# Hybrid linear-attention and sliding-window block on one core: the value product of each attention job placed one product sooner, its second bank of scores exponentiated first, and the jobs' transfers moved in the queue

## The reference

```python
h = rmsnorm(x, g_pre)
q_a, k_a, v_a, lr_a, z_a, q_b, k_b, v_b, z_b, m_a, m_b = split(h @ w_in)
# branch A, gated linear attention: 4 heads, keys of 128, values of 256, chunks of 64 tokens
log_a = log_sigmoid(lr_a @ w_decay_up + b_decay_up) / 16
for each chunk:  S = S * exp(b_last) + (k * exp(b_last - b)).T @ v;   o = q @ S      # b = cumsum(log_a)
y_a = (rmsnorm(o_a, g_gla) * silu(z_a)) @ w_branch_gla
# branch B, attention: 16 heads of 64, 2 shared key heads, window of two chunks, rope, a learned sink
p = softmax(concat(q_b @ k_b.T / 8, sink))[..., :-1];   o_b = p @ v_b
y_b = (o_b * silu(z_b)) @ w_branch_swa
y = sigmoid(m_a + b) * y_a + sigmoid(m_b + b) * y_b
x = x + rmsnorm(y @ w_out, g_post)
```

## Time and profile before

| | |
|---|---|
| median of 3 runs | 1947.06 us (1942.76 to 1947.96) |
| the profiled execution, its own time | 1943.41 us |
| its span | 1941.5 us |
| TensorE matmul busy | 1859.3 us, 96% |
| VectorE busy | 1361.9 us, 70% |
| GpSimd busy | 1022.8 us, 53% |
| ScalarE busy | 814.8 us, 42% |

### The profile page before, as it was taken

One profiled execution on the slowest core, in us unless ns is written; L12 is line 12 of the kernel. 1 busy time (PEld: TensorE's weight loads), 2 busy tenths in 40 slices (PEclk: granted clock), 3 DMA queues, 4 the chain that ended last, 5 costly groups with the idle time before them and its releaser, 6 DMA issues. The chain is left out here.

```text
span 1941.5 us, 31399 instructions
## 1 busy us (share of the span) xinstructions
PE 1859.3 (96%) x11024; PEld 1478.0 (76%) x11024; DVE 1361.9 (70%) x2140; ACT 814.8 (42%) x1808; POOL 1022.8 (53%) x673
## 2 busy tenths in 40 slices
PE   8999989989999999999999999999999999999996
PEld 7877767777777767887877777777777777887885
DVE  6768866866788876647568877755888856446265
ACT  5456455433333444313246454543443444225431
POOL 5534445554444556734534555555454467538955
PEclk9999989999999999999999999999999999999998
DMA  7534375677888777877843365666887786775873
GB/s 277 136 96 138 122 219 162 178 213 207 218 213 257 226 207 233 276 261 264 230 141 127 106 185 165 157 168 156 211 245 234 219 257 232 250 229 193 279 253 118
DMA packets 474463, 391.20 MB, mean 201 GB/s; under 512 B 292836, under 2 KB 365092, under 8 KB 460996
## 3 DMA queue, kind: packets, MB, share of 16 engines
q1 hardware_dynamic: 474307, 389.20, 67.3%
HBM read 256.45 MB, written 132.64 MB: 200 GB/s over the span
## 5 line engine op out<-in xcount | busy, mean ns | idle before, releaser
L1008 PE MATMUL pu<-a_hi,w_hi 128*128 128x512 f32 x1824 | 729.1, 402 | 30.1 <-DVE ct L1842 12.2
L1008 PE MATMUL pu<-a_lo,w_hi 128*128 128x512 f32 x1824 | 713.1, 393 | 0.0
L1008 PE MATMUL pu<-a_hi,w_lo 128*128 128x512 f32 x1824 | 712.3, 393 | 0.4 <-POOL w_lo L1991 0.4
L1991 POOL TENSOR_TENSOR w_lo<-t,w_hi 128x512 fp32r<-128x512 f32 x256 | 357.3, 1405 | 418.7 <-ACT w_hi L1327 418.7
L1991 POOL TENSOR_TENSOR w_lo<-w_raw,w_hi 128x512 fp32r<-128x512 f32 x264 | 399.8, 1524 | 268.1 <-ACT w_hi L1327 268.0
L1008 PEld LDWEIGHTS pu<-a_hi,w_hi 128*128 128x128 f32 x1824 | 345.7, 190 | 138.0 <-issue 60.2
L1008 PEld LDWEIGHTS pu<-a_hi,w_lo 128*128 128x128 f32 x1824 | 346.1, 190 | 75.5 <-POOL w_lo L1991 0.8
L1008 PEld LDWEIGHTS pu<-a_lo,w_hi 128*128 128x128 f32 x1824 | 346.4, 190 | 68.0
L1327 ACT ACTIVATE w_hi<-t 128x512 fp32r<-128x512 f32 x256 | 158.5, 628 | 356.5 <-DVE t L534 284.6
L1009 PE MATMUL pu<-a_hi,w_hi 128*128 128x512 f32 x544 | 212.2, 390 | 0.0
L1009 PE MATMUL pu<-a_hi,w_lo 128*128 128x512 f32 x544 | 211.7, 389 | 0.0
(11 more groups left out here) (177 smaller groups left out, 2336.9 us busy)
## 6 DMA issues: line engine op xcount, KB each, us to landing
w_raw<-in_w SPq DMA_DIRECT2D x81, 1024.0 KB, 6.2
va_d<-ct SPq DMA_DIRECT2D x128, 64.0 KB
qb_d<-ct SPq DMA_DIRECT2D x32, 256.0 KB
zb_d<-ct SPq DMA_DIRECT2D x32, 256.0 KB
q_s<-qb_d SPq DMA_DIRECT2D x32, 256.0 KB, 3.3
z_s<-zb_d SPq DMA_DIRECT2D x32, 256.0 KB, 3.1
gb_d<-gb SPq DMA_DIRECT2D x32, 256.0 KB, 2.9
za_d<-ct SPq DMA_DIRECT2D x128, 64.0 KB
```

Source lines behind the costliest of these rows:

```text
L1008: return nc.tensor.matmul(dst, weights, moving, start=start, stop=stop, skip_group_check=True)
L1991: TT(flat(w_lo[o.n % NWB][:, :, :]), src, as_f32(flat(w_hi[o.n % NWB][:, :, :])), ALU.subtract) \
```

## The change

In words:

1. `SWA_PV` goes from f+7 to f+6, and with it `prob_values` on TensorE and `gb` on VectorE. `SWA_Z` goes from f+5 to f+4, but `load_swa_z` now stands behind the slot's stores.
2. The exponentials of `pm[1]` are done first, and `exp_ok` counts twice a job: after `pm[1]` and after the sink. The value product waits for the first count of the next job.
3. `RB` goes from slots 92 and 96 to 90 and 94, and ScalarE's copy of it stands ahead of the exponentials.
4. In SP's loop the store of `gb` and the loads of linear attention stand at the slot's start. The store of `ga` is one slot later. Stores of `qk`, `v`, `mA`, `mB` and `out` tiles are one slot later.
5. GpSimd's multiply of `z_g` stands first in its slot, and VectorE's `ga` last in its slot.
6. The first loads of `gate_b` come up to four slots sooner, each with the waits that its buffer needs.

```diff
-SWA_Z = {first + 5: n for first, n in SWA.items()}
-SWA_PV = {first + 7: n for first, n in SWA.items()}
+SWA_Z = {first + 4: n for first, n in SWA.items()}
+SWA_PV = {first + 6: n for first, n in SWA.items()}
-RB = {92: 0, 96: 1}
+RB = {90: 0, 94: 1}
...
                 if j == 0:
-                    sp.wait_ge(rd_ok, 16 * (sb + 1))
-                    stored(group_no(sb, "mB", 3))
+                    if n == 0:
+                        stored(group_no(sb, "mB", 3))
+                        sp.wait_ge(rd_ok, 16 * sb + 15)
+                        sp.wait_ge(up_ok, 16 * sb + 16)
+                    elif n == 2:
+                        sp.wait_ge(rd_ok, 16 * (sb + 1))
...
-                if r - 10 in GLA:
-                    job = GLA[r - 10]
+                if r - 11 in GLA:
+                    job = GLA[r - 11]
...
+                if r - 2 in SWA_PV:
+                    job = SWA_PV[r - 2]
...
+                    sp.wait_ge(gb_ok, n + 1)
+                    go(gb_d[g * 512:(g + 1) * 512, t0:t0 + P].rearrange("(e p) t -> p e t", p=P), gb[:, :, :], gb_out)
+                if r + 3 in GLA:
+                    load_gla(sb, GLA[r + 3])
+                if r + 1 in GLA:
+                    load_gla_q(sb, GLA[r + 1])
+                if r - 6 in GLA:
+                    load_gla_z(sb, GLA[r - 6])
                 if r + 5 == min(SWA):
                     load_swa(sb, 0)
                 elif r + 3 in SWA and SWA[r + 3]:
                     load_swa(sb, SWA[r + 3])
                 if r - 1 in SWA:
                     load_swa_v(sb, SWA[r - 1])
-                if r in SWA_Z:
-                    load_swa_z(sb, SWA_Z[r])
-                for g, n in ((step(s, lag), n) for n, lag in ((3, 4), (0, 5), (2, 6), (1, 7))):
+                for g, n in ((step(s, lag), n) for n, lag in ((3, 5), (0, 6), (2, 7), (1, 8))):
                     if g and g.fast and g.kind in ("qk", "v", "mA", "mB", "out"):
                         store_tile(g, n)
...
+                if r in SWA_Z:
+                    load_swa_z(sb, SWA_Z[r])
...
-                if r - 1 in SWA_PV:
-                    job = SWA_PV[r - 1]
...
-                if r + 3 in GLA:
-                    load_gla(sb, GLA[r + 3])
-                if r + 1 in GLA:
-                    load_gla_q(sb, GLA[r + 1])
-                if r - 6 in GLA:
-                    load_gla_z(sb, GLA[r - 6])
...
                 for n in range(4):
-                    if e == n - 2:
+                    if e == (-6, -5, -2, -4)[n]:
                         load_gate_b(sb, 0, n)
...
             def scores(n):
-                pe.wait_ge(exp_ok, n)
+                pe.wait_ge(exp_ok, 2 * n)
...
             def prob_values(n):
-                pe.wait_ge(exp_ok, min(n + 2, 16 * (n // 16 + 1)))
+                pe.wait_ge(exp_ok, 2 * n + 3 if n % 16 < 15 else 2 * n + 2)
...
+                if sb == 0 and r in RB:
+                    act.wait_ge(rb_ok, 3 + RB[r])
+                    A(rb[:, RB[r], :], pm[4][:, :], ACT.Copy).then_inc(rb_sb_ok, 1)
                 if r in SWA:
...
-                    for hh in range(8):
-                        A(prob[b][:, :, hh, :], pm[hh // 4][:, (hh % 4) * P:(hh % 4 + 1) * P]
-                          .rearrange("p (j k) -> p j k", k=TB), ACT.Exp, bias=ntop[b][:, hh:hh + 1], scale=HD ** -0.5, accum_out=den[b][:, hh:hh + 1])
+                    for hh in (4, 5, 6, 7, 0, 1, 2, 3):
+                        ins = A(prob[b][:, :, hh, :], pm[hh // 4][:, (hh % 4) * P:(hh % 4 + 1) * P]
+                                .rearrange("p (j k) -> p j k", k=TB), ACT.Exp, bias=ntop[b][:, hh:hh + 1],
+                                scale=HD ** -0.5, accum_out=den[b][:, hh:hh + 1])
+                        if hh == 7:
+                            ins.then_inc(exp_ok, 1)
...
-                if sb == 0 and r in RB:
-                    act.wait_ge(rb_ok, 3 + RB[r])
-                    A(rb[:, RB[r], :], pm[4][:, :], ACT.Copy).then_inc(rb_sb_ok, 1)
```

More of the change, by code:

```diff
@@ L829, in _ @@
                            ga[j * TB:(j + 1) * TB, :, :], ga_out)
+                if r - 2 in SWA_PV:
+                    job = SWA_PV[r - 2]
+                    n = 16 * sb + job
+                    g, t = divmod(job, NT)
+                    t0 = sb * SB + t * P
+                    sp.wait_ge(gb_ok, n + 1)
[6 more added lines that the diff above has]
+                    load_gla_z(sb, GLA[r - 6])
                 if r + 5 == min(SWA):
@@ L1759, in _ @@
                     dve.wait_ge(ntop_ok, 2 * n + 1)
-                    dve.wait_ge(exp_ok, n)
+                    dve.wait_ge(exp_ok, 2 * n)
                     TT(sd[:, :], cs["sinks"][:, 8 * g8:8 * g8 + 8], ntop[n % 2][:, :], ALU.add).then_inc(ntop_ok, 1)
@@ L1764, in _ @@
                     d = den[n % 2]
-                    dve.wait_ge(exp_ok, n + 1)
+                    dve.wait_ge(exp_ok, 2 * n + 2)
                     link(TT(d[:, :], d[:, :], se[:, :], ALU.add))
@@ L1814, in _ @@
                     dve.wait_ge(st_ok, n + 1)
[L1815 to L1821, removed]
                 g, i = at(s)
@@ L1952, in _ @@
                     split_fill(SPLIT_AT[s])
+                if r - 9 in GLA:
+                    n = 16 * sb + GLA[r - 9]
+                    dve.wait_ge(o_t_ok, n + 1)
+                    dve.wait_ge(zg_ok, n + 1)
+                    dve.wait_ge(ga_out, 16 * NB * n)
+                    TT(ga[:, :, :].rearrange("p g t -> p (g t)"), o_n[:, :],
+                       z_g[:, :, :].rearrange("p g t -> p (g t)"), ALU.mult).then_inc(ga_ok, 1)
                 if s == NS - 2 or s == NS:
@@ L2017, in _ @@
                 sb, r = rel(s)
+                if r - 8 in GLA:
+                    n = 16 * sb + GLA[r - 8]
+                    pr = n % 16 // NT
+                    pool.wait_ge(gla_z_in, 16 * (n + 1))
+                    TT(z_g[:, :, :], z_g[:, :, :], gate_g[:, 16 * pr:16 * pr + 16].unsqueeze(2)
+                       .broadcast_to([P, 16, TB]), ALU.mult).then_inc(zg_ok, 1)
                 if s in LO_AT:
@@ L2047, in _ @@
                     p = prob[n % 2]
-                    pool.wait_ge(exp_ok, n + 1)
+                    pool.wait_ge(exp_ok, 2 * n + 2)
                     pool.wait_ge(den_ok, n + 1)
@@ L2051, in _ @@
                        .broadcast_to([P, NB, 8, TB]), ALU.mult).then_inc(p_ok, 1)
[L2052 to L2057, removed]
                 if s == NS - 1 or s == NS:
```

5 lines of the change are left out of this document (removed).

## The result

The changed kernel takes 1932.83 us (median of 6 runs, 1925.52 to 1935.68) against 1943.31 us for the kernel before (6 runs, 1939.47 to 1947.96). The ratio is 0.9942, 95% interval 0.9926 to 0.9959: 11 us faster. 29 to 33 us were forecast (1914 us against 1943 or 1947). The number lies inside the range of the prediction, beside what it called rival (a). The profiled execution took 1935.43 us, its span is 1933.6 us: 8.0 us less than before by profile.

A forecast was written before the change was run, and what follows sets the result against it. TensorE, with matmuls busy 96% of the span, and its waits were taken as the bound. Savings 14 + 0 - 3 + 14 + 6 = 31 us took 1943.41 to 1912.4; half of 3.65 added gave 1914 us, range 1896 to 1936.

The forecast's parts named there:

- rival (a): Whole kernel: VectorE and SP give back more of the gain, 7 us saved, 1938 us; chance 0.20.
- What bounds the kernel: Whole kernel: TensorE's own work, busy 96% of the span, and what keeps it waiting set the end.
- half a stretch: TensorE after longer waits: a removed wait also gives back half its half-speed work; 20.5 us lost in all.
- Linear attention: Edits 4 and 5, both blocks: `z_g` first and `ga` last put L1842 ahead; 14 us saved, bounds 5 and 19.
- The waits before slots 204 and 468: Linear attention: TensorE's waits for L1842, 3.8 and 2.9 us, would be gone.
- Attention after the first job: Edits 1 and 2, later jobs of each block: `gb` waits removed; 14 us saved, bounds 5 and 22.
- the one half-speed stretch that was allowed: Attention, 345 to 485 us: no granted clock of 0.50 there, or one stretch.
- The first job: First attention job of a block: keys late instead of `gb`; no change, bounds 5 saved in both blocks, 4 lost.
- the norm: Second block, edit 3: TensorE's spread waits 3.1 us, half-speed stretch behind; 3 us lost, bounds 0 and 5.
- yB: Gates and fills, edit 6: fill 3 to 6 us sooner, L1831 waits shrink; 6 us saved, bounds 0 and 9.
- the sign that I named for it: Later tile stores, costed at nothing: lost cover would show as VectorE waiting for `ct` stores.
- (c): Attention: the value product waits for the second bank in each of 30 jobs; slower, 1959 us; chance 0.05.

The follow-up runs named there:

- z_two: The changed kernel with two `z_g` buffers and the load of `z_g` one slot sooner, `z_g` still first in GpSimd's slot: ratio 0.9901 to the kernel before.
- zg_last: The changed kernel with GpSimd's `z_g` put back last in its slot, VectorE's `ga` left last: ratio 0.9894 to the kernel before.
- only_ga_last: The kernel before with one edit, VectorE's `ga` last in its slot: ratio 0.9940 to the kernel before.
- hx_99: The changed kernel with two `z_g` buffers and VectorE's instructions of the second block's norm one slot sooner: 1912.69 us, ratio 0.9841 to the kernel before.
- m_early: The changed kernel with the stores of `mA` and `mB` tiles put back one slot sooner: ratio 0.9951 to the kernel before.

## Why the prediction was wrong, by its steps

**What bounds the kernel.** Right: all the gains come out of TensorE's waits and its half-speed work. How a gain splits between the two differs from one execution to the next. In the profiled pair it is all clock, over all the executions mostly waits, so that the sum's habit of adding half a stretch to each removed wait can't be tested on one pair.

**Linear attention, -14 forecast, -2 measured (3.4 and -1.5 us gained): the step that failed.** The prediction put it: "`z_g` takes 1.04 us of GpSimd ahead of `w_lo`, which is needed four slots later, so it is hidden." I priced the instruction and not the wait in front of it. I had also noted that `z_g`'s load waits for `ga` of the job before "at the end of a slot now", and followed that to SP's stores but not to GpSimd. The runs showed 84.7 us of GpSimd standing in 30 waits (58.9 in 18 before), now ahead of the slot's `w_lo`; VectorE's work 5.4 and 4.2 us longer than in `z_two`, where the standing is 16.5; and ten waits for `k_g`, 12.4 us, which the prediction does not mention. The mechanism that was forecast for `ga` last is right: without `z_g` first the two stages gain 10.1 and 6.2 us in `zg_last` and 8.1 and 6.0 in `only_ga_last`, 16 and 14 together, and 14 was said. The waits before slots 204 and 468 went as said.

**Attention after the first job, -14 forecast.** By the trace 9.9 + 0.9 = 10.8; `gb` no longer waits anywhere, as said, and the one half-speed stretch that was allowed is there. It is mis-sized by the wait of 4.8 us before slot 104. That VectorE becomes the limit between 345 and 400 us was said, and priced at 5; that its instructions are 2.5 times as long beside GpSimd's was not seen, although `ga` took 1.68 us in the earlier trace rows. Timed by themselves, the edits 1 to 3 gave 5.4 us where -14 + 3 = -11 was forecast. The traces do not settle why this is less than the 8.4 that they show in the changed kernel; both carry an uncertainty of 3 us or so.

**The first job, 0; the norm, +3.** Right in size: up to slot 94 the span is 2.4 us longer. The wait of 3.3 us at slot 90 was forecast as 3.1, and the keys took `gb`'s place at slot 78. The half-speed stretch that was to follow the norm's wait is not in this profile; other profiles with the same wait have it (`zg_last` at 314.6 us, `hx_99` at 314.1). SP stood longer than I thought, until 265.52, not 260 to 263, since the `zB` store took longer to land.

**yB, -6 forecast, nothing measured.** The fill's two waits there (L1831, 2.7 and 2.6 us) fell to one of 1.2, and L1859 rose by 5.4. The later stores, costed at nothing, are the reason for the second, and the sign that I named for it (VectorE waiting for `ct` stores) is the row above. But they are not what took the 6 us: with `mA` and `mB` stored early again `m_early` was no faster.

**The rivals.** The result lies nearest to (a), 1938, whose words were that VectorE and SP give it back; VectorE did, but `z_g` first with GpSimd's wait was the trigger, and no rival named GpSimd. (c) did not come: of 30 value products three wait for the exponentials.

## What to carry to other kernels

When an instruction is moved to the front of an engine's slot, price the wait that it brings, not its own length: ask when its operand's buffer is freed, and by whom, after the other moves of the same change. A good move (`ga` last, worth some 11 us by itself) can be undone by one that looks free (`z_g` first) through one single-buffered tile; run the square of four. And when a removed wait comes back under another name three times over, the bound is a chain; look for what stretches its links. And before a gain is put down to the clock or to waits, look at the clock of more than one execution.

## What the runs showed of the hardware

- In one pair of profiles TensorE's waits stayed at 84.1 us against 82.2 and the kernel still became 8 us faster, because fewer stretches ran at 0.50 of the clock (27.2 us instead of 43.7). Executions of one and the same kernel have mean granted clocks from 0.982 to 0.989, so that a single pair can show several us of this that are not the change's.
- The same VectorE instruction with two inputs in SBUF takes 0.68 us alone and 1.76 beside a GpSimd instruction, which itself goes from 1.3 to 1.73 us; with one input in PSUM it stayed at 0.69 or less beside GpSimd. A change of order on GpSimd alone (after against `zg_last`) changed VectorE's busy time in a stage by 4.6 us at an equal count of instructions.
